# Opening of a two-block transformer kernel: zero products ahead of x, a three-pass first chunk, a conversion shared by three engines, bias rows and turns placed behind the first chunks

## The reference

```
def rmsnorm(x, g):
    y = x * rsqrt(mean(x * x) + EPS)
    return y * g
def swiglu_ffn(x, w_in, w_out):
    gate, up = split(x @ w_in, 2)          # w_in 1024 x 5632
    return (silu(gate) * up) @ w_out       # w_out 2816 x 1024
h = x + 0.5 * swiglu_ffn(rmsnorm(x, ffn1_norm[0]), ffn1_w_in[0], ffn1_w_out[0])
...
head_bias(rel) = rel_bias[rel_bucket(rel)]  # used by attention, much later
```

## Time and profile before

| | us |
|---|---|
| median of 3 runs | 1353.47 |
| lowest and highest | 1350.81, 1356.68 |
| the profiled execution | 1353.99 |
| its span | 1352.2 |
| TensorE busy | 1294.2 (96%) |
| VectorE, ScalarE, GpSimd busy | 845.9, 613.5, 533.1 |

### The profile page before, as it was taken

The page is one execution under the profiler, slowest core; times in us unless marked ns, Lnnn a source line. Parts: engine busy times, 40 slices in busy tenths (PEclk is TensorE's granted clock), DMA queues, the critical chain, the costliest instruction groups (busy, mean ns, idle before and its releaser), DMA issues.

```text
span 1352.2 us, 27527 instructions
## 1 busy us (share of the span) xinstructions
PE 1294.2 (96%) x10703; PEld 1238.6 (92%) x10703; DVE 845.9 (63%) x1353; ACT 613.5 (45%) x880; POOL 533.1 (39%) x565
## 2 busy tenths in 40 slices
PE   7999999999999998999999889999999997899878
PEld 6999999999999998999999668999999996788758
DVE  5775458786554466555556784754456685875576
ACT  5443344344333354334435675633334436434382
POOL 4555544335455433544441252555542002610043
PEclk8999999999999999999998889999999998989989
DMA  8787655657776555666644115666663453334300
GB/s 258 231 234 215 205 171 156 185 174 234 217 217 189 184 166 169 197 198 197 199 131 150 42 36 156 188 187 187 195 200 110 132 170 150 113 107 143 126 32 32
DMA packets 275122, 222.62 MB, mean 165 GB/s; under 512 B 8098, under 2 KB 256438, under 8 KB 274924
## 3 DMA queue, kind: packets, MB, share of 16 engines
q1 hardware_dynamic: 272528, 215.59, 52.2%
q0 software_dynamic: 1504, 4.49, 1.7%
q10 hardware_dynamic: 1020, 1.58, 0.3%
HBM read 216.40 MB, written 4.19 MB: 163 GB/s over the span
## 4 chain that ended last, share of the span: by engine, by line
PE 80%; DVE 10%; ACT 6%; issue 2%; POOL 1%; DMA 1%; ACTq 0%; DVEq 0%; SPq 0%; POOLq 0%
PE psum L744 24%; PE psum L746 24%; PE psum L745 24%; DVE hn_tiles L1710 2%; DVE wal L1885 1%; ACT pbuf L1491 1%; DVE wal L1692 1%; ACT hn_tiles L1305 1%; PE psum L690 1%; ACT wah L1225 1%; DVE hres L1758 1%; PE psum L974 1%; PE psum L1154 1%; ACT arena L1319 1%; DVE hn_tiles L1746 0%
## 5 line engine op out<-in xcount | busy, mean ns | idle before, releaser
L744 PE MATMUL psum<-hn_tiles,wah 128*128 128x256 f32 x2032 | 571.8, 281 | 6.3 <-DVE wal L1692 3.0
L745 PE MATMUL psum<-hn_tiles,wah 128*128 128x256 f32 x2032 | 565.4, 278 | 0.0
L746 PE MATMUL psum<-hn_tiles,wal 128*128 128x256 f32 x2032 | 565.1, 278 | 0.0
L2336 POOL TENSOR_TENSOR wbl<-raw_b,wbh 128x256 fp32r<-128x256 f32 x412 | 402.0, 1006 | 392.3 <-ACT wbh L1232 381.9
L744 PEld LDWEIGHTS psum<-hn_tiles,wah 128*128 128x128 f32 x2032 | 384.0, 189 | 12.6 <-issue 8.0
L745 PEld LDWEIGHTS psum<-hn_tiles,wah 128*128 128x128 f32 x2032 | 383.6, 189 | 1.8 <-issue 1.7
L746 PEld LDWEIGHTS psum<-hn_tiles,wal 128*128 128x128 f32 x2032 | 383.7, 189 | 0.0
L1692 DVE TENSOR_TENSOR wal<-raw_a,wah 128x2048 fp32r<-128x2048 f32 (+3 forms) x127 | 292.8, 2305 | 105.9 <-ACT wah L1225 104.8
L1225 ACT ACTIVATE wah<-raw_a 128x2048 fp32r<-128x2048 f32 (+2 forms) x125 | 235.4, 1884 | 74.3 <-PE psum L746 51.6
L1351 ACT ACTIVATE gate_hid<-tmp 128x256 f32<-128x256 f32 x88 | 36.7, 417 | 415.1 <-DVE tmp L1802 415.1
L744 PE MATMUL psum<-hidh,wbh 128*128 128x256 f32 x768 | 212.6, 277 | 0.9 <-DVE hidl L1746 0.9
(11 more groups left out here) (304 smaller groups left out, 1674.2 us busy)
## 6 DMA issues: line engine op xcount, KB each, us to landing
raw_a<-in_ffn_w_in SPq DMA_DIRECT2D x176, 512.0 KB, 5.0
raw_b<-in_ffn_w_out SPq DMA_DIRECT2D x88, 512.0 KB, 4.3
raw_a<-in_w_in_even SPq DMA_DIRECT2D x15, 1024.0 KB, 5.1
raw_a<-in_conv_w_in SPq DMA_DIRECT2D x24, 512.0 KB, 4.4
raw_a<-in_w_in_odd SPq DMA_DIRECT2D x11, 1024.0 KB, 5.2
raw_a<-in_w_kv SPq DMA_DIRECT2D x6, 1024.0 KB, 6.2
raw_b<-in_conv_w_out SPq DMA_DIRECT2D x8, 512.0 KB, 5.7
raw_a<-in_attn_w_q SPq DMA_DIRECT2D x4, 1024.0 KB, 5.1
```

The source lines that it names most:

```text
L744: mm(dst, wh, xh, start=start, stop=False)
L745: mm(dst, wh, xl, start=False, stop=False)
L746: return mm(dst, wl, xh, start=False, stop=stop)
L2336: x = g.tensor_tensor(low[:, c], full[:, c], high[:, c].bitcast(F32), ALU.subtract)
```

## The change

Nine products of zeros stand first on TensorE, into a bank that is overwritten later; VectorE clears the source (`rt`) for them as its first instruction. `opening_chunk` takes the place of `first_chunk` for the first chunk of all: high x high for all eight tiles, then high x low, then low x high, so that the low weights are wanted last. The conversion of chunk 0 is divided: ScalarE makes the high part of tiles 0 to 3, VectorE that of tiles 4 to 7 and, after all eight low gained tiles, the low part of tiles 0 to 3; GpSimd makes the low part of tiles 4 to 7, ahead of its folds. The bias row products move behind up 0 and behind down 0, the 30 turns and `rest_of_parameters` behind down 1, and what copies their results moves to tasks of chunks 0, 1 and 3. The angle tasks move two chunks later (sines and VectorE's angles and cosines). The twelve parameter loads move from ScalarE's queue to SP's, between the input weights of chunks 0 and 1 and the first output rows.

```diff
--- before.py
+++ after.py
@@ -472,6 +472,8 @@
             for tt in range(2):
                 sp.dma_start(xn[:, tt, :], a["x"][0, tt * P:(tt + 1) * P, :]).then_inc(S("x_loaded"), 16)
             load_ffn_first(0)
+            for dst, src in PARAMS[6:]:
+                sp.dma_start(dst, src).then_inc(S("params_loaded"), 16)
             load_ffn(0)
             load_conv()
 
@@ -763,16 +765,35 @@
                 c = slice(g * P, (g + 1) * P)
                 return lambda k: (wah[:, s, k, c], wal[:, s, k, c])
 
-            def first_weights(s, g):
-
-                def tiles(k):
-                    if g == 0 and k % 4 == 0:
-                        pe.wait_ge(S("first_lo"), k // 4 + 1)
-                    return weights(s, g)(k)
-
-                return tiles
-
-            def ffn(sums=True, extra=lambda: None, halves=False):
+            def opening_chunk(b):
+
+                dsts, s = [b[:, g * T:(g + 1) * T] for g in range(2)], [weights(0, g) for g in range(2)]
+                for k in range(KT):
+                    pe.wait_ge(S("gh_ready"), k + 1)
+                    if k % 4 == 0:
+                        pe.wait_ge(S(("first_hi", "later_hi")[k // 4]), 1)
+                    for g in range(2):
+                        mm(dsts[g], s[g](k)[0], hnh[:, k, :], start=k == 0 and g == 0, stop=False)
+                for k in range(KT):
+                    pe.wait_ge(S("hn_ready"), k + 1)
+                    for g in range(2):
+                        mm(dsts[g], s[g](k)[0], hnl[:, k, :], start=False, stop=False)
+                for k in range(KT):
+                    if k == 0:
+                        pe.wait_ge(S("first_lo"), 1)
+                    elif k >= 4:
+                        pe.wait_ge(S("later_lo"), k - 3)
+                    for g in range(2):
+                        m = mm(dsts[g], s[g](k)[1], hnh[:, k, :], start=False, stop=k == KT - 1 and g == 1)
+                n["hn"] += KT
+                return m
+
+            def keep_busy(b, count, stationary, moving):
+
+                for _ in range(count):
+                    mm(b[:, 0:512], stationary, moving, start=True, stop=True)
+
+            def ffn(sums=True, extra=lambda: None, halves=False, behind=()):
 
                 def up(i, u):
                     if not (halves and i is FIRST and u == 0):
@@ -782,9 +803,9 @@
                     s, at = (n["sa"] + u) % 2, 4 + (n["ffn"] + u) % 2
                     b = bank[at]
                     if i is FIRST and u == 0:
-                        first_chunk([b[:, g * T:(g + 1) * T] for g in range(2)],
-                                    [(first_weights if halves else weights)(s, g) for g in range(2)]
-                                    ).then_inc(S("gu_ready"), 1)
+                        (opening_chunk(b) if halves else
+                         first_chunk([b[:, g * T:(g + 1) * T] for g in range(2)], [weights(s, g) for g in range(2)])
+                         ).then_inc(S("gu_ready"), 1)
                         return
                     for g in range(2):
                         c = slice(g * P, (g + 1) * P)
@@ -802,6 +823,8 @@
                         pe.wait_ge(S("copy_ready"), n["copy"])
                     hs = (n["hid"] + u) % 2
                     add_rows(i, u, hidh[:, hs, :], hidl[:, hs, :], FC, first=i is FIRST and u == 0)
+                    if i is FIRST and behind:
+                        behind[u]()
 
                 def after_first():
                     if sums:
@@ -977,6 +1000,9 @@
                         x.then_inc(S("pv_done"), 1)
 
 
+            zeros = rt[:, :].bitcast(BF16)
+            pe.wait_ge(S("zeros_ready"), 1)
+            keep_busy(bank[4], 9, zeros[:, 0:P], zeros[:, 0:512])
             pe.wait_ge(S("const_loaded"), 16)
             pe.wait_ge(S("gains_loaded"), 16)
             pe.transpose(bank[6][:, 0:16], vecs[0:16, 0, :], cst[0:16, C_ID:C_ID + 16]).then_inc(S("par_turned"), 1)
@@ -987,30 +1013,41 @@
                         x = pe.transpose(bank[j][:, t * T + tt * P:t * T + (tt + 1) * P],
                                          xn[:, tt, (2 * j + t) * P:(2 * j + t + 1) * P], ident)
                 x.then_inc(S("xt_ready"), 1)
-            pe.wait_ge(S("onehot_loaded"), 32)
-            pe.wait_ge(S("rb_one"), 1)
-            mm(bank[7][0:16, 0:EW], rb[:, :], onehot[:, 0:EW], start=True, stop=True).then_inc(S("rows_ready"), 1)
-            mm(bank[5][0:16, 0:EW], rb[:, :], onehot[:, EW:2 * EW], start=True, stop=True).then_inc(S("rows_ready"), 1)
-            pe.wait_ge(S("par_ready"), 1)
-            pe.wait_ge(S("turned_rows_copied"), 1)
-            for i in range(2):
-                for b in range(NC):
-                    at = EW + 224 + P * i - 16 * b
-                    x = pe.transpose(bank[6][:, (i * NC + b) * 16:(i * NC + b + 1) * 16], frow[0:16, at:at + P],
-                                     cst[0:16, C_ID:C_ID + 16])
-            x.then_inc(S("bias_ready"), 1)
-            pe.wait_ge(S("bias_copied"), 1)
+
+            def rows(half):
+
+                if half == 0:
+                    pe.wait_ge(S("onehot_loaded"), 32)
+                    pe.wait_ge(S("rb_one"), 1)
+                else:
+                    pe.wait_ge(S("rt_ready"), n["rn"])
+                mm(bank[6 + half][0:16, 0:EW], rb[:, :], onehot[:, half * EW:(half + 1) * EW], start=True, stop=True
+                   ).then_inc(S("rows_ready"), 1)
+
+            def compressed_biases():
+
+                pe.wait_ge(S("bias_copied"), 1)
+                pe.wait_ge(S("turned_rows_copied"), 1)
+                for i in range(2):
+                    for b in range(NC):
+                        at = EW + 224 + P * i - 16 * b
+                        x = pe.transpose(bank[6][:, (i * NC + b) * 16:(i * NC + b + 1) * 16], frow[0:16, at:at + P],
+                                         cst[0:16, C_ID:C_ID + 16])
+                x.then_inc(S("bias_ready"), 1)
 
             def rest_of_parameters():
 
                 pe.wait_ge(S("params_loaded"), 16 * (NPAR - 6))
                 pe.wait_ge(S("norms_loaded"), 16 * (6 - NGAIN))
-                pe.wait_ge(S("tcmp_copied"), 1)
-                pe.transpose(bank[6][:, 0:120], vecs[0:120, 0, :], cst[0:120, C_ID:C_ID + 120])
-                pe.transpose(bank[6][:, 128:160], vecs[0:32, 1, :], cst[0:32, C_ID:C_ID + 32]
+                pe.transpose(bank[7][:, 0:120], vecs[0:120, 0, :], cst[0:120, C_ID:C_ID + 120])
+                pe.transpose(bank[7][:, 128:160], vecs[0:32, 1, :], cst[0:32, C_ID:C_ID + 32]
                              ).then_inc(S("par_turned"), 1)
 
-            ffn(extra=rest_of_parameters, halves=True)
+            def last_openings():
+                compressed_biases()
+                rest_of_parameters()
+
+            ffn(extra=lambda: rows(0), halves=True, behind=(lambda: rows(1), last_openings))
             conv()
             ffn()
 
@@ -1500,22 +1537,14 @@
                 wait_residual(t)
                 gained(G_FFN1_0, t)
             wa.wait_loaded(act, 0, 0, 2)
-            for half in range(2):
-                k = slice(4 * half, 4 * half + 4)
-                x = act.activation(wah[:, 0, k, :], raw_a[:, 0, k, :], ACT.Copy)
-                x.then_inc(S("first_hi"), 1)
-            act.wait_ge(S("rows_ready"), 1)
-            act.activation(frow[0:16, 0:EW], bank[7][0:16, 0:EW], ACT.Copy, scale=1.0 / SQRT_D
-                           ).then_inc(S("bias_copied"), 1)
+            act.activation(wah[:, 0, 0:4, :], raw_a[:, 0, 0:4, :], ACT.Copy).then_inc(S("first_hi"), 1)
             for j in range(4):
                 square_residual(j)
             load_root()
             n["res"] += 1
-            act.wait_ge(S("first_hi"), 2)
+            act.wait_ge(S("first_hi"), 1)
             act.sem_inc(S("a_hi"), 1)
             hi_first("ffn", 1)
-            for dst, src in PARAMS[6:]:
-                act.dma_start(dst, src).then_inc(S("params_loaded"), 16)
             act.dma_start(cst[:, C_BLK:C_W], a["consts"][:, C_BLK:C_W]).then_inc(S("rest_loaded"), 16)
             act.dma_start(posi[:, :], a["positions_2"].to_broadcast([P, T])).then_inc(S("rest_loaded"), 16)
 
@@ -1524,11 +1553,17 @@
                 act.activation(rope[:, 2 * i, :], angles[i], ACT.Sin, scale=0.5)
                 act.activation(rope[:, 2 * i + 1, :], angles[i], ACT.Sin).then_inc(S("sin_ready"), 1)
 
+            def copy_rows():
+                act.wait_ge(S("rows_ready"), 1)
+                act.activation(frow[0:16, 0:EW], bank[6][0:16, 0:EW], ACT.Copy, scale=1.0 / SQRT_D
+                               ).then_inc(S("bias_copied"), 1)
+
             def copy_compressed_biases():
                 act.wait_ge(S("bias_ready"), 1)
                 act.activation(tcmp[:, 0:480], bank[6][:, 0:480], ACT.Copy).then_inc(S("tcmp_copied"), 1)
 
-            ffn(G_FFN1_0, "conv", tasks={4: lambda: sines(0), 5: lambda: sines(1)}, first=copy_compressed_biases, root_first=True)
```

(41 more changed lines are left out.)

## The result

The kernel became slower: 1361.06 us in the median of 20 runs (1354.98 to 1366.31), against 1351.84 for the kernel before (20 runs, 1348.95 to 1356.68). The ratio, taken over all runs and not from the medians, is 1.006, 95% interval 1.0048 to 1.0072; the plain difference of the medians is 9.2 us. The 20 runs of after fall into two groups with a hole between them, 8 at 1354.98 to 1357.40 (median 1356.7) and 12 at 1359.58 to 1366.31 (median 1362.5). The profiled execution took 1364.27 us (span 1362.5), 10.3 more than the profiled one of before.

The account below looks back on a forecast made before the run. TensorE, busy 96% of the span, was taken as the bound. Chunk 2 earlier (-2.5 us) plus turns still owed (+2.3) gave -0.2, 1353.3 against the median; with a clock fall weighed in, 1353.5 us, range 1348.5 to 1358.5.

Parts of the forecast that it names:

- Zeros, first product, VectorE's high half: Opening: zeros give 0.3 us, clock likely down again by the first product at 12.0; VectorE's high half takes 0.7 us.
- rival D: Opening: zeros keep the clock full (0) or it stays half through the first chunk (+0.3 us); chance 0.64, with the forecast.
- Low tiles at 0.53 us each: VectorE's eight low tiles of chunk 0 at 0.53 us each, then a low half of 1.74; buffer released at 17.4.
- First chunk ends at 19.2: TensorE's first chunk takes 7.2 us as before, between 5.5 at full clock and 9.5, and ends at 19.2.
- Chunk 2's load landed at 23, hidden tile at 28.4: Chunk 2's load takes 4.7 us to land; hidden tile comes at 27.5 to 29.3, so TensorE waits 1.4 us.
- Chunk 2 at 32.0: TensorE starts chunk 2 at 32.0, 2.5 us ahead of before (1.6 to 3.4).
- Turns and parameters 2.3: Behind down 1, the 30 turns and the parameters' two still owed take 2.3 us (2.1 to 3.8).
- SP's small loads, 1 us at most: Twelve small loads on SP delay the first rows; ScalarE may wait 1 us, under cover: cost 0, without cover 1.
- Rival C, the clock falls again: Behind down 1's 32 turns the clock falls: 1356.5 us, or 1358 with a second fall; chance 0.15.

Follow-up runs that it names:

- a_no_zeros: The changed kernel without the nine zero products; 1357.86 us median of 7 runs, ratio 1.0029 to the kernel before.
- b_rows_moved: The kernel before with only the bias rows, 30 turns and parameter turns moved behind the chunks' products; 1354.12 us median of 12 runs, ratio 1.0013.
- a_rows_back: The changed kernel with row products, 30 turns and parameter turns back where the kernel before has them; 1354.76 us median of 12 runs, ratio 1.0016.
- a_lows_dve: The changed kernel with GpSimd's four low pieces of chunk 0 given to VectorE; 1363.19 us median of 6 runs, ratio 1.0078 to the kernel before.
- a_params_act: The changed kernel with the twelve parameter loads back on ScalarE's queue, ahead of the constants; 1370.99 us median of 4 runs, ratio 1.012.
- after_again: The changed kernel unaltered, run once more for another profile; 1362.17 us in one run.
- after_beside: The changed kernel unaltered, timed in another series; 1362.62 us median of 6 runs, ratio 1.0081 to the kernel before.
- a_pause: The changed kernel with TensorE's second chunk pair written out and a wait ahead of down 2; 1360.15 us median of 10 runs, ratio 1.0049.
- a_unroll: The changed kernel with one more chunk pair written out, so the loop begins 17 us behind the turns; 1361.98 us median of 5 runs, ratio 1.0073.
- b_release_unroll: The kernel before with chunk 0's buffer released early, 30 turns in the second FFN's wait and a chunk pair written out; 1355.54 us, ratio 1.0032.
- b_release_early: The kernel before with chunk 0's buffer released early, 30 turns in the second FFN's wait, parameter turns behind down 1; 1352.51 us, ratio 0.9998.
- b_entry_break: The kernel before with the two parameter turns repeated directly ahead of the first FFN's loop; 1353.74 us median of 12 runs, ratio 1.0021.

## Why the prediction was wrong

- *Zeros, first product, VectorE's high half.* Right: x's turns in 2.59 instead of 3.33, first product 12.16 (12.0), the cast 0.69 (0.7), clock down again at 10.8. In a_no_zeros the first product is 0.6 later (0.3 forecast), and nothing of it is left at chunk 2. Neither case of rival D came: the clock was at half for the first 5.4 us of the chunk and full behind it.
- *Low tiles at 0.53 us each: the term that failed first.* It was read from the mean of four of which GpSimd's fold overlapped only the last one. In b_rows_moved four tiles took 0.42 each without GpSimd and 0.78 with it, in after 0.83. Eight are 6.6 us and not 4.2: the release came at 19.8, not 17.4. The Trainium skill, "GPSIMD Engine Reference", section "Key points", says that VectorE and GpSimd contend where VectorE has two SBUF inputs; the trace agrees (0.42 against 0.83), and I had cited the rule and yet priced the tiles by a mixed mean.
- *First chunk ends at 19.2.* It ended at 22.0: the same low half, late by 2.4, left a gap of 1.18 us, and half clock lasted 2.1 us longer within the chunk than before. (The range's upper end, 9.5 us, was also too low for a chunk all at half clock: 48 products at the 0.21 us of the working are 10.1.) The folds did end early (18.7, forecast 19.9), but the sum of squares, put at half a microsecond behind them, had to wait for the chunk and took 1.8: it ended at 23.6, not 20.5.
- *Chunk 2's load landed at 23, hidden tile at 28.4: the step that decides chunk 2's start.* Landed 26.96, tile at 32.50. The load was issued 2.5 us late, by the release, and its second half took 6.3 us where I had put 4.9. The 4.7 of the earlier trace rows is the median of two, 4.0 for the first half and 5.3 for the second, which is the one that counts. The sum let 0 to 1 us of overlap with the constants stand for all other loads and left out that the first output rows, moved from 8.94 to 16.00, would still be under way (landed 22.59). In a_rows_back and a_lows_dve an earlier release did not mend it, and how the 4.0 us divide between release and moved loads stays open. The wait of TensorE was 2.2 (1.4 forecast) although chunk 1 too began 3.2 late.
- *Chunk 2 at 32.0.* Measured 36.4: the lead of 2.5 became a debt of 1.9. I had written that a start after 34 would prove it wrong.
- *Turns and parameters 2.3.* Right: 44.98 to 47.38 is 2.40.
- *SP's small loads, 1 us at most.* ScalarE waited 5.84 for the first rows. Chunk 2's load, later still, hid that wait, so it cost nothing by itself; whether the rows' later transfer is part of what made chunk 2's load late was not tested, and cost 0 is not shown. a_params_act shows only what the old place costs when the constants follow on the same queue.
- *Rival C, the clock falls behind the turns.* It did in the first profile (1.00 in the turns, 0.50 from 48.3 to 51.7) and did not in after_again and after_beside. The Trainium skill, "TensorE: Matmul & The Clock Gate", section "Part 4: PE-mode transpose", says that transposes don't count as activity; a fall 1.3 us behind them agrees, and so do nine of twelve profiles with the 30 turns in that place; three without a fall, two of them of after itself, say that it is not certain. Its price was forecast as 1.7; by chunk 4's start it is about 1.3. The wait for the hidden tile is no sure sign either: 2.2 us were followed by a fall in a_pause and by none in after.
- *What no step had: the pace.* The sum that the rows now give at chunk 4 is +6.55 with the fall and about +5.2 without, which is the lower group (+4.8). The slow pace's 5.8 us on top make the upper one. I had taken a busy TensorE at 1.00 as one speed. The median of the lower group, 1356.7, lies inside the forecast's range, that of the upper one, 1362.5, outside it: the late chunk 2 spoils the sum, and the pace takes the time out of the range.

What sets the pace stays open. Shown is that it lasts through the loop, that it differs between executions of one program, and that a fall of the clock is neither needed for it (after_again) nor a cure (after has both). How often it comes differs. Of the 18 profiled executions with small products behind down 1 (the 30 turns, the two of the parameters, or both) eight show it, among them all three of after; of the two with none there (before, a_rows_back) neither does. The times of single runs say the same less surely: after has 12 of 20 in its upper group, a_unroll 3 of 5, b_release_unroll 6 of 12, b_release_early 4 of 11, b_entry_break 3 of 12, and a_rows_back has no run over 1356.80; but the kernel before once reached 1358.05 in 27 runs, and a_pause and b_rows_moved have runs at the top of their range with the quick pace. That points to small products in the running stream as what gives the slow pace its chance. It was only counted, the places where it begins fit it, and no run shows why one execution takes it up and the next does not.

## What to carry to other kernels

Before pricing an instruction by the mean of a group, look at what the other engine did in each part of it: the mean of a half-overlapped group fits neither case. When a first chunk is started earlier, follow the release of its buffer and the other loads that are on their way when it comes. If the next load does not land earlier, work set behind the chunk is added and not hidden, and a load moved out of one engine's way can stand in another load's. And when TensorE is busy at full clock in both traces, count the products in an equal stretch before you look for the loss elsewhere.

## What the runs showed of the hardware

- At a granted clock of 1.00 and without a wait, 256-column products with a weight load each start every 113.3 ns or every 117.8 ns, and a loop keeps one of the two for 150 us. The Trainium skill, "TensorE: Matmul & The Clock Gate", section "Wait — 56ns, not 53.3ns?", gives columns by 2.4 GHz plus about 2.5 ns for matmuls back to back, an estimate of 109.2 ns for 256 columns, and names no second pace; both measured ones lie above it, in a stream with a weight load for each product, and the measurement decides.
- A VectorE operation with two SBUF inputs took 0.42 us alone and 0.78 to 0.83 beside GpSimd; GpSimd's subtraction of 128x256 took 0.88 there and 0.69 beside an idle VectorE (VectorE beside an idle GpSimd: 0.35). Which of the two is held up differs: in a_rows_back four of VectorE's tiles took 1.65 us, and GpSimd's four folds beside them 7.47 instead of 3.55.
- What else is loading sets when a load lands: with the constants (1153 KB) issued at 19.8 instead of 14.9, right ahead of it, chunk 2's load landed at 31.79 instead of 26.96 (a_params_act, which has the small loads elsewhere too).
- 30 small turns in 2.0 us within a busy stream were followed by a fall to half clock in nine of twelve profiled executions, 0.1 to 1.4 us behind the last turn, and by none in three.
